# Latent heads packed four to three 128-row blocks, their scores as six products in pairs

## The reference

```python
q = (rms_norm(c_q, q_norm_g) @ w_uq).reshape(b, s, MLA_HEADS, MLA_NOPE + MLA_ROPE)   # 8 heads, 64 + 32
kv = (rms_norm(c_kv, kv_norm_g) @ w_ukv).reshape(b, s, MLA_HEADS, MLA_NOPE + MLA_V)
if rope is not None:                      # latent tokens only
    q_rope = rope_2d(q_rope, rope)
    k_r = rope_2d(k_r, rope)
q = jnp.concatenate([q_nope, q_rope], axis=-1)
k = jnp.concatenate([k_nope, jnp.broadcast_to(k_r, (b, s, MLA_HEADS, MLA_ROPE))], axis=-1)
s = jnp.einsum('bqhd,bkhd->bhqk', q, k).astype(jnp.float32) * scale
p = jax.nn.softmax(s, axis=-1)
```

## Time and profile before

| | us |
|---|---|
| median of 3 runs | 1522.17 (1520.7 to 1522.53) |
| profiled launch | 1524.24 |
| its span, first to last instruction | 1522.4 |
| PE busy in it | 1431.9 (94%) |
| DVE, ACT, POOL busy | 706.6, 374.1, 170.9 |
| latent attention, layer 0 | from 235 to 367 |
| latent attention, layer 1 | from 1068.6 to 1125 |

### The profile page before, as it was taken

One profiled execution on the slowest core, in us unless ns is written; L12 is line 12 of the kernel. 1 busy time (PEld: TensorE's weight loads), 2 busy tenths in 40 slices (PEclk: granted clock), 3 DMA queues, 4 the chain that ended last, 5 costly groups with the idle time before them and its releaser, 6 DMA issues.

```text
span 1522.4 us, 19421 instructions
## 1 busy us (share of the span) xinstructions
PE 1431.9 (94%) x7718; PEld 820.1 (54%) x7718; DVE 706.6 (46%) x1584; ACT 374.1 (25%) x810; POOL 170.9 (11%) x118
## 2 busy tenths in 40 slices
PE   6999999999999999989997888999999999999786
PEld 3343344554444445665544437654677885766453
DVE  2568954444335963433111116796454443444222
ACT  4111404433223012212221115230443202100001
POOL 0010521000001120012221110133000110000000
PEclk9999999999999999999999899999999999999999
DMA  9422422121212346289999978631233468899996
GB/s 383 197 111 111 200 111 111 56 84 56 84 56 110 118 202 274 92 331 415 418 418 420 414 301 354 244 119 56 67 113 139 166 256 334 346 420 420 420 421 272
DMA packets 50765, 350.78 MB, mean 230 GB/s; under 512 B 8160, under 2 KB 8672, under 8 KB 17904
## 3 DMA queue, kind: packets, MB, share of 16 engines
q1 hardware_dynamic: 45072, 338.99, 55.5%
q0 software_dynamic: 5024, 8.40, 1.5%
q10 hardware_dynamic: 576, 2.10, 0.3%
HBM read 346.57 MB, written 11.80 MB: 235 GB/s over the span
## 4 chain that ended last, share of the span: by engine, by line
PE 78%; SPq 9%; DMA 7%; DVE 3%; ACT 2%; issue 1%; DVEq 0%; ACTq 0%
PE bank L384 74%; DMA arena<-w_up_in 7%; SPq L2664 4%; ACT arena L1181 2%; SPq L2673 2%; SPq L2653 2%; PE bank L721 2%; PE bank L475 1%; PE bank L1076 1%; DVE arena L1619 1%; DMA x<-x_in 0%; PE bank L840 0%; PE bank L1092 0%; DVE am L1901 0%; DVE arena L1916 0%
## 5 line engine op out<-in xcount | busy, mean ns | idle before, releaser
L384 PE MATMUL bank<-arena 128*128 128x512 f32 (+10 forms) x6104 | 1259.0, 449 | 48.4 <-DMA arena<-w_up_in 39.6
L384 PEld LDWEIGHTS bank<-arena 128*128 128x128 f32 (+4 forms) x6104 | 670.0, 161 | 538.9 <-issue 415.7
L1181 ACT ACTIVATE arena<-bank 128x512 f32<-128x512 f32 (+5 forms) x434 | 209.0, 500 | 972.8 <-PE bank L384 863.8
L1619 DVE SCALAR_TENSOR_TENSOR arena<-arena,bank 64x256 f32<-64x256 f32 (+2 forms) x121 | 58.0, 480 | 334.2 <-ACT arena L1181 232.9
L1619 DVE SCALAR_TENSOR_TENSOR arena<-arena,vec 128x512 f32<-128x512 f32 (+1 forms) x254 | 175.8, 765 | 0.4
L1901 DVE TENSOR_REDUCE am<-bank 128x1 f32<-128x512 f32 (+1 forms) x96 | 55.6, 600 | 165.7 <-PE bank L384 165.7
L2488 POOL TENSOR_TENSOR arena<-arena 128x512 f32<-128x512 f32 (+1 forms) x32 | 38.2, 1195 | 434.1 <-DVE arena L1619 434.1
L1181 ACT ACTIVATE arena<-bank,am 128x512 f32<-128x512 f32 (+1 forms) x96 | 58.6, 613 | 67.1 <-DVE am L1904 67.0
L2527 POOL DMA_INDIRECT y<-arena,routing x33 | 32.9, 997 | 189.8 <-ACT arena L1181 185.1
L721 PEld LDWEIGHTS bank<-con,arena 128*128 128x128 f32 x240 | 29.8, 141 | 34.4 <-issue 22.7
L1963 DVE SCALAR_TENSOR_TENSOR arena<-arena 128x1024 f32<-128x1024 f32 x32 | 45.4, 1434 | 5.9 <-DMA arena<-adaT_in 5.8
(11 more groups left out here) (189 smaller groups left out, 739.2 us busy)
## 6 DMA issues: line engine op xcount, KB each, us to landing
arena<-w_down_in SPq DMA_DIRECT2D x65, 1024.0 KB
arena<-w_gate_in SPq DMA_DIRECT2D x61, 1024.0 KB
arena<-w_up_in SPq DMA_DIRECT2D x61, 1024.0 KB
arena<-ada_in SPq DMA_DIRECT2D x16, 2048.0 KB, 9.5
arena<-mg_in SPq DMA_DIRECT2D x12, 2048.0 KB, 8.1
arena<-adaT_in SPq DMA_DIRECT2D x16, 1024.0 KB, 8.0
arena<-mo_in SPq DMA_DIRECT2D x6, 2048.0 KB, 8.0
arena<-glu_in SPq DMA_DIRECT2D x4, 2048.0 KB, 13.5
```

The lines of the kernel that those rows point to most:

```text
L384: return nc.tensor.matmul(out, w, rhs, start=start, stop=stop)
L1181: return nc.scalar.activation(out, in_, fn, **kw)
L1619: return V.scalar_tensor_tensor(out, in0, sc, in1, op0=op0, op1=op1)
```

## The change

The queries and keys of four heads lie in three blocks of 128 rows instead of four blocks of 96. With the heads named 0 to 3: block 0 holds head 0 whole in rows 0 to 95 and the rotated rows of head 1 in rows 96 to 127; block 1 holds the own rows of head 1 (0 to 63) and of head 2 (64 to 127); block 2 holds head 3 whole in rows 0 to 95 and the rotated rows of head 2 in rows 96 to 127. The host permutes the weights' columns to match (`NOPE_ORDER`, `ROPE_ORDER`), and the cosine and sine tables are repeated on 64 rows.

The units run over four heads before the next query tile. Their scores are six products in place of four, issued in three calls: at the first unit 96 rows and then 32 rows, the latter opening the next unit's bank; at the second 64 and 64 rows, one closing its own bank and one opening the next; at the third 32 rows, then 96 rows that are the fourth unit's whole score; the fourth issues nothing.

```diff
-        qa = grid(arena[:, 0:4096], HA)
-        oa = qa[:, 0:8:2, :]
+        qa = grid(arena[:, 0:3072], 6)
...
+        def oa_of(pair):
+            return qa[:, 3 * (pair // 2) + pair % 2, :]
...
-            return ([(2 * p + j, t, seen[t]) for p in range(HA // 2) for t in tiles for j in range(2)],
+            return ([(4 * g + j, t, seen[t]) for g in range(HA // 4) for t in tiles for j in range(4)],
...
-                end("a", mm(ps[64:96, 0:T], con_at("pick"), P[:, 3, :], True, True))
+                for r in (64, 96):
+                    last = mm(ps[r:r + 32, 0:T], con_at("pick"), P[:, 3, :], True, True)
+                end("a", last)
...
-                    ins = mm(bank_of[("branch", l, c, b)][:, 0:T - q0], w[:, c, k, :], (oa, cv, qd)[MERGE[b]][:, k, q0:T], k == 0, k == 3)
+                    ins = mm(bank_of[("branch", l, c, b)][:, 0:T - q0], w[:, c, k, :], (cv[:, k, :], oa_of(k), qd[:, k, :])[b][:, q0:T], k == 0, k == 3)
...
-                    if u >= 4:
-                        pe.wait_ge(s["exp_ready"], u - 3)
-                    mm(PS[2 + u % 4][:, 0:nk], qa[0:96, i, t * 128:t * 128 + 128], ka[0:96, i, 0:nk], True, True) \
-                        .then_inc(s["scores"], 1)
+                    j, g = i % 4, 3 * (i // 4)
+
+                    def part(v, b, r0, r1, start, stop):
+                        return mm(PS[2 + v % 4][:, 0:nk], qa[r0:r1, g + b, t * 128:t * 128 + 128], ka[r0:r1, g + b, 0:nk], start, stop)
+
+                    if j == 3:
+                        return
+                    if u >= 3:
+                        pe.wait_ge(s["exp_ready"], u - 2)
+                    if j == 0:
+                        part(u, 0, 0, 96, True, True).then_inc(s["scores"], 1)
+                        part(u + 1, 0, 96, 128, True, False)
+                    elif j == 1:
+                        part(u, 1, 0, 64, False, True).then_inc(s["scores"], 1)
+                        part(u + 1, 1, 64, 128, True, False)
+                    else:
+                        part(u, 2, 96, 128, False, True).then_inc(s["scores"], 1)
+                        part(u + 1, 2, 0, 96, True, True).then_inc(s["scores"], 1)
...
-                give(f(lora[64:96, 3, :], ps[64:96, :], ACT.Copy))
+                give(f(lora[64:128, 3, :], ps[64:128, :], ACT.Copy))
...
+                def by_heads(to, ps, i, cols, n):
+                    g = 3 * (i // 2)
+                    if i % 2:
+                        give(f(to[:, g + 1, cols], ps[:, 0:n], ACT.Copy))
+                    else:
+                        f(to[0:64, g, cols], ps[0:64, 0:n], ACT.Copy)
+                        give(f(to[0:64, g + 2, cols], ps[64:128, 0:n], ACT.Copy))
...
+                    by_heads(qa, take(("uq", l, i)), i, slice(q0, T), NQ)
                 for i in range(2):
                     ps = take(("uq", l, 4 + i))
-                    for j in range(4):
-                        ins = f(qa[64:96, 4 * i + j, q0:T], ps[32 * j:32 * j + 32, 0:NQ], ACT.Copy)
-                    give(ins)
+                    f(qa[64:128, 3 * i, q0:T], ps[64:128, 0:NQ], ACT.Copy)
+                    give(f(qa[64:128, 3 * i + 2, q0:T], ps[0:64, 0:NQ], ACT.Copy))
                 for i in range(4):
-                    ps = take(("uk", l, i))
-                    f(ka[0:64, 2 * i, :], ps[0:64, :], ACT.Copy)
-                    give(f(ka[0:64, 2 * i + 1, :], ps[64:128, :], ACT.Copy))
+                    by_heads(ka, take(("uk", l, i)), i, slice(0, T), T)
...
-                V.stream_shuffle(Pq, qa[64:96, :, CTX:T], swap).then_inc(s["rope_part"], 1)
+                for b in range(2):
+                    ins = V.stream_shuffle(P[64:128, b, :].rearrange("p (g n) -> p g n", g=2), qa[64:128, 2 * b:6:3, CTX:T], swap)
+                ins.then_inc(s["rope_part"], 1)
...
-                G.tensor_copy(ka[64:96, :, :], lora[64:96, 3:4, :].to_broadcast([32, HA, T])).then_inc(s["pool_set"], 1)
+                for b in (0, 2):
+                    ins = G.tensor_copy(ka[64:128, b:6:3, :], lora[64:128, 3:4, :].to_broadcast([64, 2, T]))
+                ins.then_inc(s["pool_set"], 1)
...
-                rotate(2, (64, 96), qa, Pq, "cos_a", "sin_a", HA)
...
+                rotate(2, (64, 128), [(qa[:, 2 * b:6:3, :], P[64:128, b, :].rearrange("p (g n) -> p g n", g=2)) for b in range(2)],
+                       "cos_a", "sin_a", 2)
```

More of the change, by code:

```diff
@@ L2451, in _, with rotate @@
                     pool.wait_ge(empty["d"], Dn[("adaT",) + units[n][1:]])
-                G.tensor_copy(ka[64:96, :, :], lora[64:96, 3:4, :].to_broadcast([32, HA, T])).then_inc(s["pool_set"], 1)
+                for b in (0, 2):
+                    ins = G.tensor_copy(ka[64:128, b:6:3, :], lora[64:128, 3:4, :].to_broadcast([64, 2, T]))
+                ins.then_inc(s["pool_set"], 1)
                 pool.wait_ge(s["pool_set"], seen(l, "pool_set", 2))
-                def rotate(part, rows, q, t, cos, sin, heads):
+                def rotate(part, rows, parts, cos, sin, heads):
@@ L2457, in rotate @@
                     pool.wait_ge(s["rope_part"], seen(l, "rope_part", part))
                     r = slice(*rows)
-                    if sin is not None:
-                        step(G.tensor_tensor(t, t, con_at(sin)[r, :].unsqueeze(1).to_broadcast([rows[1] - rows[0], heads, SEQ]), op=MUL))
-                    step(G.tensor_tensor(q[r, :, CTX:T], q[r, :, CTX:T],
-                                         con_at(cos)[r, :].unsqueeze(1).to_broadcast([rows[1] - rows[0], heads, SEQ]), op=MUL))
-                    pool.wait_ge(pool_step, own[0])
@@ L2464, in rotate @@
-                    G.tensor_tensor(q[r, :, CTX:T], q[r, :, CTX:T], t, op=ADD).then_inc(s["rope_pool"], 1)
+                    for q, t in parts:
+                        if sin is not None:
+                            step(G.tensor_tensor(t, t, con_at(sin)[r, :].unsqueeze(1).to_broadcast([rows[1] - rows[0], heads, SEQ]), op=MUL))
+                        step(G.tensor_tensor(q[r, :, CTX:T], q[r, :, CTX:T],
+                                             con_at(cos)[r, :].unsqueeze(1).to_broadcast([rows[1] - rows[0], heads, SEQ]), op=MUL))
+                        ins = G.tensor_tensor(q[r, :, CTX:T], q[r, :, CTX:T], t, op=ADD)
@@ L2786, in tables @@
         else:
-            con[rows:rows + 32, CON[c][0]:CON[c][1]] = np.concatenate([cos] * 2)
-            con[rows:rows + 32, CON[s_][0]:CON[s_][1]] = np.concatenate([-sin, sin])
+            con[rows:rows + 64, CON[c][0]:CON[c][1]] = np.concatenate([cos] * 4)
+            con[rows:rows + 64, CON[s_][0]:CON[s_][1]] = np.concatenate([-sin, sin] * 2)
     r = np.zeros((128, NRC), np.float32)
```

26 lines of the change are left out of this document (12 added, 14 removed).

## The result

The changed kernel took 1535.65 us, the median of four launches (1532.64 to 1538.07), beside 1522.06 us for the kernel before on the same chip (1520.70 to 1522.53): a ratio of 1.0094, 95% interval 1.0080 to 1.0108. The forecast was 1539.1 with a range of 1531 to 1545. The profiled launch took 1536.21 us, 12.0 more than the profiled launch before, where the sum gave 16.9.

A forecast was written before the change was run, and what follows sets the result against it. PE was taken to set the pace in latent attention. Score products and shape changes, +20.4 us, less 2.85 of waits and 0.59 of ACT's copies, gave +16.9 and a forecast of 1539.1 us, range 1536 to 1544.5 (1531 to 1545 with the third rival).

The forecast's parts named there:

- the sum: Whole kernel: +20.4 us for score products, less 2.85 for PE's waits and 0.59 for ACT's copies, +16.9 us.
- The mechanism: Latent attention scores: 96- and 32-row products run one after the other, with 0.20 us per change of shape; chance 0.78.
- The first two rivals: Scores: 96 and 32 rows run together, without change cost (1517.5 us, chance 0.11) or paying it (1522.3 us, 0.05).
- The third rival: Scores: 96 and 32 rows run one after the other, no change cost between them, only streaming; 1531.9 us, chance 0.06.
- Layer 0's stage: Layer 0's latent attention: longer by some 12.1 us, 13.0 less 0.64 and 0.30 of absorbed waits.
- second-`turn` wait: PE's idle before the second `turn`, 1.17 us in layer 0 and 1.57 in layer 1, shrinks to about 0.5.
- ACT's copies: Projections: 16 copies for 24 remove PE's one wait on ACT in layer 0, -0.59 us; none in layer 1.
- Layer 1's stage: Layer 1's latent attention: longer by some 5.5 us, 7.4 less 1.07, 0.40 and 0.44 of absorbed waits.
- the later waits: PE's waits where convolution work delays DVE or ACT, 0.30 us in layer 0, 0.54 and 0.44 in layer 1; 0.30, 0.40, 0.44 absorbed.
- the 0.44: One of layer 1's later PE waits in latent attention, beside convolution work: counted as absorbed in full, 0.44 us.
- the 0.54: Layer 1's later PE wait whose preceding step loses its score: 0.40 us of its 0.54 counted as absorbed.
- the danger: Attention steps without a score open new waits, PE having 0.87 us less there: 0.2 us for 12 steps, 2.4 us.

The follow-up runs named there:

- 64-beside-32 kernel: The changed kernel with each 96-row product cut to rows 0 to 63, so its pair is 64 and 32 rows on disjoint strips: 1580.29 us, one launch.

## Why the prediction was right, and where it was not

**The mechanism held.** The 96- and the 32-row product run one after the other. The records' starts show it, leaving the 32-row products out gave their price, and equal heights in their place removed most of the loss. The first two rivals are out: on disjoint rows 64 and 32 start 0.52 us apart, 32 and 32 within 0.01. The third rival, no change between 96 and 32 rows, is out by the same starts: 1.05 us for the product and the change, not 0.86. The Trainium skill's "TensorE: Matmul & The Clock Gate", Part 3, has products in distinct row groups run concurrently and names no condition on their heights. In the 64-beside-32 kernel they don't (0.52 us apart), and the measurement decides. The Trainium skill's "TensorEngine Tiling (Array Packing)", Tiling Modes, has modes of 128, 64 and 32 rows and a drain between them. The runs agree with it, a 96-row product behaving as one of 128, and the price of a change here is 0.20 us.

**The terms of the sum.** Layer 0's stage grew by 11.7 for 12.1, its second-`turn` wait shrank to 0.54 for about 0.5, and the new order of the units cost nothing, as the sum had it.

**ACT's copies were mis-sized**: 0.59 us taken, 3.8 measured between the two kernels and 3.7 with the copies put back. The step that failed is "PE waits for it once in layer 0 ... none in layer 1". It read PE's idle time; the waits were in the weight loads, and PE's records hid them.

**Layer 1's stage grew by 7.4 for 5.5.** One term of the sum was mis-sized: of the later waits the 0.44 was absorbed, but the 0.54, counted as 0.40 back, grew by 0.5, which makes 0.9. The other 1.7 us is no term of the sum: 3.4 us at half clock, which not even the launches of one attention program have in the same place. Against them stand 0.7 us less that I haven't traced. The prediction named the danger (a step without a score opens a wait) and priced it at 0.2 us per step for its range; the one place where it happened was where DVE had the convolution as well.

**Not forecast: the clock elsewhere.** Two stretches that the change doesn't touch ran with less time at half clock. Before:

```profile
905.00:930.00 25.00, 18.30 (x116) 12.15 (x112) 11.69 (x20) 12.19 (x24) 3.52 (x3) 0.80 0.82 324
...
1287.00:1299.00 12.00, 12.00 (x66) 12.00 (x66) 4.91 (x24) 4.58 (x10) 0.00 (x0) 0.57 1.01 423
```

The same work after:

```profile
913.00:938.00 25.00, 16.72 (x121) 11.25 (x121) 12.07 (x22) 12.87 (x26) 3.98 (x3) 0.93 0.77 311
...
1299.00:1311.00 12.00, 9.44 (x69) 9.09 (x70) 5.72 (x27) 5.96 (x14) 0.00 (x0) 0.86 1.01 427
```

The granted clock is 0.93 for 0.80 and 0.86 for 0.57, and across these two stretches the shift falls by 1.5 and 2.2 us, which is less than the 3.4 us that the clock alone would give in either (6.8 us less at half clock): within each the shift goes lower and comes partly back. With the 0.8 us of the start this is 4.5 us that the forecast didn't have and that nothing in the change explains. In the launch with the copies put back the start was 1.0 us late, not 0.8 early; and around the router the twelve profiled launches have from none to 13.7 us at half clock, long and short with the change and without. Why it differs from launch to launch stays open; I made no run for it. Against the forecast of 1541.2 for the profiled launch, the account is -0.4 and +1.9 for the stages, -3.2 for ACT, -3.7 for the two stretches, -0.8 for the start, and +1.2 elsewhere (0.8 of it ahead of 905 us, 0.4 behind 1299), which I haven't traced: -5.0. So the launch's nearness to the forecast owes something to errors that cancel, and to luck. The stages came to 19.1 us for 17.6, of which the half clock is 1.7: at full clock they would stand at 17.4.

## What to carry to other kernels

Products that are to share TensorE must have the same height as well as disjoint rows; packing rows into full blocks pays only if it takes products away at full height, and each product on 64 or 32 rows among full ones adds its own stream and 0.20 us on either side. Read PE by the distance between the starts of its records and by the waits of its weight loads: both told of a loss, 3.8 us in all, that its idle time showed as 0.6. Where a step loses PE work, look for what else ran in its shadow: a wait of 0.54 us doubled there. And compare stages at the same granted clock: 3.4 us at half clock cost 1.7 us, as much as several of the edits here, and came to a stage that nobody had edited.

## What the runs showed of the hardware

- Products of unequal height don't overlap, even on disjoint rows and with each on a shape that pairs with its like: 64 beside 32 rows start 0.52 us apart.
- A 96-row product has no change of shape towards 128 rows, on entering or on leaving, and the full change (0.20 us) towards 32.
- A product that closes a bank and one that opens another pair as any two do (32 and 32 rows within 0.01 us, 64 and 64 "x2").
- A short wait of PE doesn't decide its clock. A wait of 1.05 us that ended at 1120.31 was followed by 3.4 us at 1.2 GHz from 1122.54 in the launch of the change, but by a clock of 1.00 with the copies put back and without the 32-row products; waits of 1.17 and 1.57 us in the kernel before left it at 1.00 too.
- A stretch of 3.4 us at 1.2 GHz costs a stage that PE fills 1.7 us: layer 0's stage took 145.87 us with one and 144.21 without, on the same products.
